# Scores over a paged latent cache: half of the cache columns transposed by VectorE in 32x32 blocks instead of by TensorE

## The reference

```python
def latent_scores(q_lat, q_pe, c, k_pe):
    s = jnp.einsum('bqhc,bkc->bhqk', q_lat, c) + jnp.einsum('bqhr,bkr->bhqk', q_pe, k_pe)
    return s.astype(jnp.float32) * MLA_SCALE

def sample_attention(q_lat, q_pe, c_new, kpe_new, c_past, kpe_past):
    T = q_lat.shape[1]
    P = c_past.shape[1]
    s_past = latent_scores(q_lat, q_pe, c_past, kpe_past)
    ...
    p = jax.nn.softmax(jnp.concatenate([s_past, s_new], axis=-1), axis=-1).astype(c_new.dtype)
    return jnp.einsum('bhqk,bkc->bqhc', p[..., :P], c_past) + jnp.einsum('bhqk,bkc->bqhc', p[..., P:], c_new)
```

## Time and profile before

| | |
|---|---|
| median of 3 runs | 1028.34 us (1028.11 to 1030.12) |
| profiled execution | 1032.82 us |
| its span in the profile | 1030.9 us |
| busy over the span | PE 95%, PEld 82%, DVE 49%, ACT 43%, POOL 15% |
| mean granted TensorE clock | 0.984 |
| the cache stage | 407.6 to about 568 us |

### The profile page before, as it was taken

One profiled execution on the slowest core, in us unless ns is written; L12 is line 12 of the kernel. 1 busy time (PEld: TensorE's weight loads), 2 busy tenths in 40 slices (PEclk: granted clock), 3 DMA queues, 4 the chain that ended last, 5 costly groups with the idle time before them and its releaser, 6 DMA issues.

```text
span 1030.9 us, 20604 instructions
## 1 busy us (share of the span) xinstructions
PE 982.4 (95%) x8588; PEld 846.4 (82%) x8588; DVE 506.8 (49%) x992; ACT 445.0 (43%) x963; POOL 157.9 (15%) x257
## 2 busy tenths in 40 slices
PE   4999999999989999899999899999999999999997
PEld 4988899877757556566665799999999999999996
DVE  5665867565475485354444532633343234334423
ACT  5545637566646676344444423431232134113312
POOL 1020500255511201344541000000000000000000
PEclk9999969999999999999999899999999999999999
DMA  7312111220024501577772321422222222222302
GB/s 247 122 46 83 43 42 42 62 48 11 2 68 113 208 1 37 195 238 267 237 241 90 109 83 41 144 82 83 87 102 99 82 83 82 83 86 98 105 1 88
DMA packets 31655, 102.58 MB, mean 100 GB/s; under 512 B 14023, under 2 KB 14967, under 8 KB 25218
## 3 DMA queue, kind: packets, MB, share of 16 engines
q1 hardware_dynamic: 22346, 63.50, 18.7%
q0 software_dynamic: 9216, 37.75, 10.7%
HBM read 96.45 MB, written 4.22 MB: 98 GB/s over the span
## 4 chain that ended last, share of the span: by engine, by line
PE 87%; DVE 6%; ACT 3%; issue 2%; DMA 1%; SPq 0%; DVEq 0%; ACTq 0%
PE PS L589 17%; PE PS L591 17%; PE PS L590 17%; PE PS L1078 7%; PE PS L1089 3%; PE PS L1113 3%; PE PS L724 2%; PE PS L1096 2%; PE PS L797 1%; PE PS L828 1%; PE PS L880 1%; PE PS L979 1%; PE PS L571 1%; DMA RAW<-in_w_stream 1%; PE PS L698 1%
## 5 line engine op out<-in xcount | busy, mean ns | idle before, releaser
L589 PE MATMUL PS<-XH,WH 128*128 128x272 f32 (+1 forms) x928 | 271.4, 292 | 1.8 <-DVE WL L1721 1.8
L591 PE MATMUL PS<-XH,WL 128*128 128x272 f32 (+1 forms) x928 | 270.3, 291 | 0.0
L590 PE MATMUL PS<-XL,WH 128*128 128x272 f32 (+1 forms) x928 | 269.5, 290 | 0.0
L589 PEld LDWEIGHTS PS<-XH,WH 128*128 128x128 f32 x928 | 175.9, 190 | 6.8 <-issue 4.2
L590 PEld LDWEIGHTS PS<-XL,WH 128*128 128x128 f32 x928 | 176.2, 190 | 0.0
L591 PEld LDWEIGHTS PS<-XH,WL 128*128 128x128 f32 x928 | 175.9, 190 | 0.0
L1222 ACT ACTIVATE WH<-RAW 128x2048 fp32r<-128x2048 f32 x46 | 88.0, 1913 | 203.1 <-PE PS L591 203.1
L589 PE MATMUL PS<-NH,WH 128*128 128x272 f32 x512 | 149.1, 291 | 0.8 <-DVE WL L1721 0.8
L591 PE MATMUL PS<-NH,WL 128*128 128x272 f32 x512 | 147.6, 288 | 0.0
L590 PE MATMUL PS<-NL,WH 128*128 128x272 f32 x512 | 146.6, 286 | 0.0
L1721 DVE TENSOR_TENSOR WL<-RAW,WH 128x2048 fp32r<-128x2048 f32 (+1 forms) x48 | 108.1, 2252 | 64.6 <-ACT WH L1222 64.2
(11 more groups left out here) (323 smaller groups left out, 1473.0 us busy)
## 6 DMA issues: line engine op xcount, KB each, us to landing
RAW<-in_w_stream SPq DMA_DIRECT2D x47, 1024.0 KB, 4.8
XN<-in_hin SPq DMA_DIRECT2D x4, 512.0 KB, 6.2
out_y_p<-YO SPq DMA_DIRECT2D x4, 512.0 KB, 2.7
CST<-in_big SPq DMA_DIRECT2D x1, 1132.5 KB, 12.8
SS<-in_sstate SPq DMA_DIRECT2D x1, 1024.0 KB, 5.1
out_ssm_s<-SS SPq DMA_DIRECT2D x4, 256.0 KB
CN<-in_cache,IDX POOLq DMA_INDIRECT x64
WQN<-in_wq SPq DMA_DIRECT2D x3, 256.0 KB, 5.8
```

The lines of the kernel that those rows point to most:

```text
L589: pe.matmul(PS[:, b, 0:n], wh, xh[:, k, c:c + n], start=(k == 0), stop=False)
L590: pe.matmul(PS[:, b, 0:n], wh, xl[:, k, c:c + n], start=False, stop=False)
L591: last = pe.matmul(PS[:, b, 0:n], wl, xh[:, k, c:c + n], start=False, stop=(k == DT - 1))
```

## The change

Only the cache stage changes.

- TensorE transposes only the first 128 latents of each row: 4 groups a unit, in two banks (4 and 7), all copied by ScalarE to CT[b].
- The other 128 latents and the 32 rope values (5 blocks of 32 columns) are transposed by VectorE within 32 x 32 blocks, one instruction per sample, from CN straight to `CB[b]`. A block transposition keeps each group q of 32 partitions to itself, so CB has 32 columns of the row on the 32 partitions of group q, for the keys of group q only.
- The scores of key group q go to bank q (banks 0 to 3, 128 keys each). `block_scores` makes 5 x 4 x 4 products (column block x, key group q, sample b) with contraction 32 and 32 columns of weights; `column_scores` makes 4 x 4 products with contraction 128. Both add into the same banks. Only one set of score banks is there now.
- The queries for the block scores must lie on every group of 32 partitions: SP lays QS out of QF and QRF with 32 small DMAs, ahead of the stage.
- pack_rope and KRN go. gather(n) still waits for the values of unit n-4.
- The maximum reads four banks at once and writes the new running maximum into SME, so two of its small instructions go; ScalarE takes the correction factor after the exponential.
- The values of a unit are computed in two halves, each behind two groups of transposes.

```diff
+            def block_scores(n):
+
+                if n >= 1:
+                    pe.wait_ge(sem("ce_exp"), n)
+                pe.wait_ge(sem("cb_done"), 4 * n + 4)
+                for x in range(5):
+                    for q in range(4):
+                        rows = slice(32 * q, 32 * q + 32)
+                        for b in range(4):
+                            heads = slice(32 * b, 32 * b + 32)
+                            last = pe.matmul(PS[heads, q, 0:P], QS[rows, n // 8, x, heads],
+                                             CB[b][rows, x, :, :].rearrange("p j k -> p (j k)"), start=(x == 0), stop=False)
                 last.then_inc(sem("ct_used"), 1)
...
+            def column_scores(n):
+
+                pe.wait_ge(sem("ct_copied"), 4 * n + 4)
+                for q in range(4):
+                    for b in range(4):
+                        heads = slice(32 * b, 32 * b + 32)
+                        last = pe.matmul(PS[heads, q, 0:P], QF[:, n // 8, 0, heads], CT[b][:, :, 32 * q:32 * q + 32],
+                                         start=False, stop=True)
+                last.then_inc(sem("ct_used"), 1)
...
+            for b in range(4):
+                cache_transposes(0, b)
+            for n in range(17):
+                if n >= 1:
+                    cache_p(n - 1)
+                if n < 16:
+                    block_scores(n)
+                    column_scores(n)
+                for half in range(2):
+                    if n + 1 < 16:
+                        cache_transposes(n + 1, 2 * half)
+                        cache_transposes(n + 1, 2 * half + 1)
+                    if n >= 1:
+                        cache_values(n - 1, half)
...
+            def block_transpose(n, b):
+                if b == 0:
+                    dve.wait_ge(sem(f"cn_in{n % 4}"), 64 * (n // 4 + 1))
+                    if n >= 1:
+                        dve.wait_ge(sem("ct_used"), 2 * n - 1)
+                dve.transpose(CB[b][:, :, :, :].rearrange("p x j k -> p j x k"),
+                              CN[n % 4][b][:, :, P:].rearrange("p j (x c) -> p j x c", c=32)).then_inc(sem("cb_done"), 1)
...
-            pack_rope(0)
-            pack_rope(1)
             pool.wait_ge(sem("pv_done"), NT_)
             gather(2)
             gather(3)
-            for n in range(2, 16):
-                if n >= 3 and n + 1 < 16:
-                    pool.wait_ge(sem("ce_pv"), n - 2)
-                    gather(n + 1)
-                pack_rope(n)
+            for n in range(4, 16):
+                pool.wait_ge(sem("ce_pv"), n - 3)
+                gather(n)
```

More of the change, by code:

```diff
@@ L295, in build @@
     ACC, at = put("ACC", [P, 2, KV], F32, at)
[L296 removed]
+    SME, at = put("SME", [P, 3, 4], F32, at)
     ML, at = put("ML", [P, 2, 4], F32, at)
@@ L307, in build @@
     assert cn_at[1][2] + rows_of <= w_at + 4 * DT * WC * 4
-    CT, at = [None] * 9, x_at
-    for i in range(9):
-        CT[i], at = put(f"CT{i}", [P, 512], F32, at)
+    CT, CB, at = [None] * 4, [None] * 4, x_at
+    for b in range(4):
+        CT[b], at = put(f"CT{b}", [P, 4, P], F32, at)
+        CB[b], at = put(f"CB{b}", [P, 5, 4, 32], F32, at)
     assert at <= x_at + 4 * 4 * (KV + DR) * 4
@@ L1075, in cache_transposes @@
                     pe.wait_ge(sem(f"cn_in{n % 4}"), 64 * (n // 4 + 1))
                 for j in range(4):
-                    src = CN[n % 4][u % 4][:, j, P * (u // 4):P * (u // 4) + P] if u < 8 else KRN[n % 2][:, j, :, :]
-                    last = pe.transpose(PS[:, CT_BANKS[x % 4], P * j:P * j + P], src, ident)
+                    last = pe.transpose(PS[:, 4 + 3 * (x % 2), P * j:P * j + P], CN[n % 4][b][:, j, 0:P], ident)
                 last.then_inc(sem("ct_mm"), 1)
-            def cache_scores(n, c):
-                if c == 0 and n >= 2:
-                    pe.wait_ge(sem("ce_exp"), n - 1)
-                g, bank = n // 8, 3 + n % 2
-                for b in range(4):
-                    wait_copied(pe, n, 4 * c + b)
-                for b in range(4):
-                    last = pe.matmul(PS[32 * b:32 * b + 32, bank, :], QF[:, g, c, 32 * b:32 * b + 32], CT[4 * c + b][:, :],
-                                     start=(c == 0), stop=False)
-                last.then_inc(sem("ct_used"), 1)
@@ L1660, in _ @@
+            for b in range(4):
+                cache_copy(0, b)
+            for n in range(17):
+                if n >= 1:
+                    cache_copy_p(n - 1)
+                for b in range(2):
+                    if n + 1 < 16:
+                        cache_copy(n + 1, b)
+                if n < 16:
+                    cache_exp(n)
+                for b in range(2, 4):
+                    if n + 1 < 16:
+                        cache_copy(n + 1, b)
             for d in range(PAIRS):
@@ L2337, in _ @@
             gather(1)
-            def pack_rope(n):
-                if n >= 2:
-                    pool.wait_ge(sem("ct_mm"), 9 * (n - 1))
-                pool.wait_ge(sem(f"cn_in{n % 4}"), 64 * (n // 4 + 1))
-                for b in range(4):
-                    last = pool.tensor_copy(KRN[n % 2][:, :, b, :], CN[n % 4][b][:, :, KV:KV + DR])
-                last.then_inc(sem("kr_packed"), 1)
-            pack_rope(0)
-            pack_rope(1)
             pool.wait_ge(sem("pv_done"), NT_)
```

151 lines of the change are left out of this document (66 added, 85 removed).

## The result

The changed kernel took 1038.72 us (median of 8 runs, 1032.96 to 1044.57), the kernel before 1028.50 in the same comparison (8 runs, 1026.98 to 1030.12). The ratio is 1.0094, with a 95% interval of 1.0067 to 1.0121. Forecast were 993 us and a range up to 1014: the sign was wrong. The profiled execution took 1035.56 us (span 1033.2) against 1032.82 before. So the two traces lie 2.7 us apart where the medians lie 10.2 apart: they show where the gain went, and not the last 7 us.

A forecast was written before the change was run, and what follows sets the result against it. TensorE alone was taken to bound the stage; afterwards the gather loop, 7.7 us a unit against TensorE's 7.51, would set the pace: stage 125.5 instead of 160.45 us, -35.0, so 993 us, range 981 to 1014.

The forecast's parts named there:

- Sum for a unit: 7.51 us: TensorE's work in one unit of the cache stage after the change, against 9.58 us before.
- 95.2 + 16 B: Time of the whole cache stage in us if block scores are slow; the kernel is slower from 4.1 us on.
- B: Block scores on TensorE: 160 records at 10.9 ns, 1.75 us a unit plus 0.10 for the turn; bounds 1.1 to 4.4.
- Case (e): Block-score records start farther apart than 10.9 ns; at 25 ns they take 4.0 us, change -1.2 us, 1027 us; chance 0.03.
- (d): Row groups of the block scores take turns: 4.4 us, period 10.16, kernel slower by 5.2 us, 1033 us; chance 0.12.
- P, C, T, V: TensorE's probability transposes, column scores, and transpose pairs with value halves: 0.54, 1.00 and 4.12 us a unit.
- The gather loop: Values, gather issue, landing, transposes: two periods at least 0.38 + 10.98 + 4.12 = 15.5 us, so 7.7 us sets the pace.
- Rival (a): Gathers faster under load, block scores near 1.1 us: 7.1 us a period, -44.3 us, 984 us; chance 0.13.
- VectorE: Four block transposes of 640 elements a partition in each unit, 0.87 us each, hidden; bounds 0.62 to 1.48 us.
- (b): VectorE's block transposes at 2.31 ns an element: 8.75 us a period, -19.9 us, 1008 us; chance 0.12.
- SP's 32 small DMAs: Laying QS out takes 10 us from about 342 us on, TensorE asks at 407: hidden, nil.
- (c): Waits for gathers bring back the half clock in the stage: 9.1 us a period, -15 us, 1013 us; chance 0.08.

The follow-up runs named there:

- no_gathers: Changed kernel with the gathers of units 4 to 15, and the waits for them, left out: 1018.64 us, 0.9901 of the kernel before.
- plain_loads: Changed kernel with units 4 to 15 loaded by SyncE's plain DMAs of fixed rows instead of GpSimd's gathers: 1058.10 us, 1.0230 of the kernel before.
- one_block: Changed kernel making the block scores of only one column block of five: 1000.89 us, 0.9713 of the kernel before.
- the burst: Kernel before with 80 tiny products added to each unit ahead of the values: 1078.51 us, ratio 1.0482; on another chip 1084.07 us, 1.0506.
- rope_no_gathers: Kernel before with only rope keys block-transposed by VectorE, latents through TensorE, and gathers of units 4 to 15 left out: 1026.68 us, ratio 0.9918.
- half_keys: Changed kernel with four of five column blocks of the block scores on 64 of 128 keys: 1084.19 us, 1.0488 of the kernel before.
- values_first: Changed kernel with both halves of a unit's values ahead of all four transpositions of the next: 1082.32 us, 1.0475 of the kernel before.

## Why the prediction was wrong, point by point

- **The step that failed**: "Sum for a unit: 7.51 us" took TensorE's time as a sum of groups whose instructions are always there. Supply had no term in it. On the chip of the result that costs 1.64 us a unit (10.0 - 8.36), 26 us over the stage; some 0.3 of it is the half clock behind two of the stops (see below), an estimate from groups at either clock. By the prediction's own 95.2 + 16 B, a B of 2.71 alone would have given 138.6 - 160.45 = -21.9, about 1006 us and inside the range: the sign went with the stops. No rival had it. Case (e) came nearest, since it too is about many instructions, but it put the price on the distance between starts.
- **B, mis-sized**: 1.85 us with its turn forecast, 2.71 measured, 16.7 ns a record in steady state where the earlier trace rows gave 10.9. The prediction read that row as tiles of 32 x 32; it says 128*32, so it has no row tiles, and 32 columns where B has 128: its rate was carried over to another kind of product. In 14 of the 16 units the first 32 records of B, two for each of the 16 tiles, start within 0.23 us, 7 ns apart but for one step of 34. So row and column tiles do work beside each other, and (d), row groups in turn, falls. What is slower is the steady rate of starts, and 64 columns do not quicken it. Of the 0.86 us, 0.46 go with GpSimd's issue of the gathers (2.25 in `no_gathers` and, beside plain DMAs, in `plain_loads`). Case (e)'s 25 ns was not reached either: 7 to 17 ns speak against that rule of the Trainium skill ("TensorE: Matmul & The Clock Gate", Part 1).
- **P, C, T, V**: 0.54, 1.00 and 4.12 forecast, 0.59, 1.01 and 4.05 measured. Right.
- **The gather loop**: 7.7 forecast as the pace. It is the floor (7.87 in `one_block`), but it did not bind. Rival (a), faster gathers, is refuted by the same run.
- **VectorE**: 0.87 forecast, 0.82 measured, and never late; (b) falls. From the page, section 5:

```profile
L2184 DVE STREAM_TRANSPOSE CB<-CN 128x640 f32<-128x640 f32 x64 | 50.0, 821 | 61.0 <-PE PS L1084 61.0
```

  That is 1.28 ns an element. The estimate from the Trainium skill's rate ("Vector Engine (DVE) Microarchitecture Reference", section 3.8), one element a cycle a lane, lay at the fast end, and this row does not bear it out for these views.
- **SP's 32 small DMAs**: landed before they were asked for, nil as said.
- **The clock**, (c): two drops in the stage beside the first (424.1 to 430.8 and 509.4 to 512.7 us), both behind stops of TensorE. A part of (c), as a consequence and not a cause. At 0.50, C took 1.87 us for 1.01, two transpose groups 1.90 for 1.02, half the values 1.77 for 1.00; both drops cost some 4.5 us, an estimate from such groups:

```profile
417.30:424.00 6.70, 3.25 (x127) 2.72 (x128) 0.60 (x1) 1.58 (x4) 0.00 (x0) 1.00 0.75 304
424.10:430.80 6.70, 6.59 (x101) 4.33 (x100) 3.90 (x6) 2.03 (x5) 0.00 (x0) 0.50 0.02 4
```

Together: a period of 10.0 instead of 7.7 is 2.3 us x 16 = 37 us, and the profiled execution took 1035.6 where 997.8 was forecast, 38 more. Of the 2.3, 0.86 are B, 1.64 the stops with the clock behind them, and -0.2 the loop that no longer binds. By the medians it is 1038.7 against 993, 46 more; the other 8 no trace here shows.

What stays open: why a packet is asked for so late, or in time as behind 503 us in `no_gathers`; why it costs 1.2 to 1.6 us more after it has landed; and what in GpSimd's issue holds TensorE's instructions and its signals back on four of the five chips of the experiments. That the stops are a lack of instructions is inferred from their spacing, from their fixed distance to the packets and from the burst; no row names it.

## What to carry to other kernels

Count TensorE's instructions in a change, weight loads included, beside its time. At 37 or 38 a microsecond no run here stopped (`rope_no_gathers`, `one_block`); at 58, or with a burst of 320 in 1.65 us, allow 1 to 3 us for each 500. Before small tiles replace large ones, look at what runs beside them: while GpSimd issues indirect gathers, put what has few instructions into that window, such as full transpositions. And time a change on several chips before its sign is trusted, when it raises the number of instructions.

## What the runs showed of the hardware that was not expected

- Records of products on 32*32 tiles start 7 ns apart in the first 32 (two for each of 16 tiles), and then 14 (2.25 us for 160) to 17 ns apart (2.71, beside GpSimd's gathers) on the mean. The pattern is the same for 64 columns as for 128.
- With 488 instructions in 8.4 us (58 a microsecond) TensorE stops for 0.6 to 3.0 us at every 254th or 127th product record, and for up to 4.6 us beside plain DMAs of another queue. With 328 in 8.9 us and no gathers (`rope_no_gathers`) it never does, nor with 232 in 6.1 (`one_block`) or 180 in 9.58; and with 488 in 7.9 it does not from 503 to 548 us of `no_gathers`. From the asking for a 16 KB packet to the next product it is 2.2 to 3.0 us at every stop.
- On four of five chips, in the changed kernel and in `half_keys`, TensorE starts 90 instructions from the start of a unit's gather issue, then some 12 in 0.72 us, until 0.9 to 1.0 us behind its end; in `values_first`, where they come later, 107 to 115 pass first. The kernel before, with 95 in that window, keeps its pace, and its time differs between the chips by only 0.5% (1028.6 and 1034).
